# Part of the modulation's row sums of blocks 1 and 3: on GpSimd instead of TensorE

## The reference, cut to what matters

```
c_act = silu(c)                                   # 1024 values
mod = c_act @ w_ada + b_ada                       # w_ada: 1024 x 3072
shift, scale, gate = split(mod, 3)
u = layer_norm(x) * (1 + scale) + shift           # 512 x 1024
proj = u @ w_in + b_in                            # 1024 x 12288
```

## Time and profile before

| | us |
|---|---|
| median of 3 runs | 2165.53 (2165.42 to 2165.72) |
| profiled execution | 2165.25 |
| its span, first to last instruction | 2163.4 |
| PE busy in the span | 2140.2 (99%) |
| DVE busy | 1274.0 (59%) |
| POOL busy | 26.6 (1%), 41 instructions |

### The profile page before, as it was taken

How to read it: one execution, slowest core, us unless ns; L and a number is a source line. 1 busy time by engine, 2 the same in 40 slices (tenths; PEclk the granted TensorE clock), 3 DMA queues, 4 the chain that set the end, 5 groups by cost and what they waited for, 6 DMA issues and landing times.

```text
span 2163.4 us, 24967 instructions
## 1 busy us (share of the span) xinstructions
PE 2140.2 (99%) x10347; PEld 1765.4 (82%) x10347; DVE 1274.0 (59%) x1675; ACT 784.8 (36%) x1044; POOL 26.6 (1%) x41
## 2 busy tenths in 40 slices
PE   7999999999999999999999999999999999999998
PEld 4888888888888887888888888888788888888887
DVE  6899897944665848435665554234843576555423
ACT  3323232223343354344343333135534435333312
POOL 1000000000000100000000000000000000000000
PEclk9999999999999999999999999999999999999999
DMA  9432232332232222322223232222232222323322
GB/s 317 145 117 83 98 103 83 98 117 98 98 102 98 98 78 78 125 71 93 83 86 109 82 113 98 88 75 91 78 121 75 88 88 81 113 80 111 103 88 78
DMA packets 181588, 217.86 MB, mean 101 GB/s; under 512 B 3932, under 2 KB 153188, under 8 KB 181220
## 3 DMA queue, kind: packets, MB, share of 16 engines
q1 hardware_dynamic: 178080, 209.47, 29.0%
q10 hardware_dynamic: 2948, 4.65, 0.6%
q0 software_dynamic: 448, 2.15, 0.3%
HBM read 212.06 MB, written 4.19 MB: 100 GB/s over the span
## 4 chain that ended last, share of the span: by engine, by line
PE 94%; DVE 4%; issue 1%; ACT 1%; DMA 0%; POOL 0%; SPq 0%; POOLq 0%; ACTq 0%; DVEq 0%
PE psum L1821 30%; PE psum L1823 29%; PE psum L1822 29%; DVE whl L518 1%; PE psum L2236 1%; PE psum L2268 1%; PE psum L1964 1%; PE psum L2248 1%; PE psum L2202 1%; DMA ada<-in_w_ada 0%; PE psum L2189 0%; PE psum L2221 0%; PE psum L1845 0%; DVE mrow L1701 0%; POOL stat L682 0%
## 5 line engine op out<-in xcount | busy, mean ns | idle before, releaser
L1821 PE MATMUL psum<-hT,whl 128*128 128x512 f32 (+1 forms) x2064 | 789.2, 382 | 2.7 <-DVE whl L518 1.5
L1823 PE MATMUL psum<-hT,whl 128*128 128x512 f32 (+1 forms) x2064 | 783.2, 379 | 0.0
L1822 PE MATMUL psum<-hT,whl 128*128 128x512 f32 (+1 forms) x2064 | 783.0, 379 | 0.0
L518 DVE TENSOR_TENSOR whl<-raw,whl 128x1024 fp32r<-128x1024 f32 x361 | 438.4, 1217 | 428.3 <-ACT whl L511 428.1
L511 ACT ACTIVATE whl<-raw 128x1024 fp32r<-128x1024 f32 x361 | 376.6, 1047 | 421.8 <-PE psum L1823 387.0
L1821 PEld LDWEIGHTS psum<-hT,whl 128*128 128x128 f32 x2064 | 388.2, 188 | 84.5 <-issue 8.1
L1823 PEld LDWEIGHTS psum<-hT,whl 128*128 128x128 f32 x2064 | 388.2, 188 | 73.5
L1822 PEld LDWEIGHTS psum<-hT,whl 128*128 128x128 f32 x2064 | 388.3, 188 | 71.8 <-issue 0.2
L1821 PE MATMUL psum<-whl,ff 128*128 128x512 f32 x352 | 137.1, 389 | 0.0
L1823 PE MATMUL psum<-whl,ff 128*128 128x512 f32 x352 | 136.9, 389 | 0.0
L1822 PE MATMUL psum<-whl,ff 128*128 128x512 f32 x352 | 136.9, 389 | 0.0
(11 more groups left out here) (327 smaller groups left out, 2156.7 us busy)
## 6 DMA issues: line engine op xcount, KB each, us to landing
raw<-in_w_in SPq DMA_DIRECT2D x87, 1024.0 KB, 5.0
raw<-in_w_up SPq DMA_DIRECT2D x44, 1024.0 KB, 5.0
raw<-in_w_down SPq DMA_DIRECT2D x20, 1024.0 KB, 5.0
raw<-in_w_branch SPq DMA_DIRECT2D x12, 1024.0 KB, 5.1
raw<-in_w_out SPq DMA_DIRECT2D x12, 1024.0 KB, 5.0
ada<-in_w_ada SPq DMA_DIRECT2D x8, 1024.0 KB, 9.6
ada<-in_w_ada SPq DMA_DIRECT2D x8, 512.0 KB, 11.1
x<-in_x SPq DMA_DIRECT2D x4, 512.0 KB, 5.3
```

The lines of the kernel that those rows point to most:

```text
L518: nc.vector.tensor_tensor(whl_view(w, 1), raw_view(w), whl_view(w, 0).bitcast(F), ALU.subtract).then_inc(w_lo, 1)
L1821: M(out_, stat_hi, mov_hi, start=start, stop=False, **kw)
L1822: M(out_, stat_hi, mov_lo, start=False, stop=False, **kw)
L1823: return M(out_, stat_lo, mov_hi, start=False, stop=stop, **kw)
```

## The change

The two or three leading row blocks of blocks 1 and 3 are no longer multiplied on PE. POOL scales each by its column of `cact` and adds them up in a new tile, `pool_part` (128x512), at a place in the arena that nothing uses at this time. It does so right after L686. The first row block is scaled into `pool_part`, the others in place, and each is then added to it; POOL waits for each of its instructions before the next. DVE adds the whole tile to its own partial sums. POOL waits for DVE's addition of block 1 before it overwrites `pool_part` for block 3. Blocks 0 and 2 stay as they are.

```
-    PE_ROWS = {0: 3, 2: 4, 1: 2, 3: 3}
+    PE_ROWS = {0: 3, 2: 4}
+    POOL_ROWS = {1: 2, 3: 3}
+    LEAD_ROWS = {**PE_ROWS, **POOL_ROWS}
...
+    pool_part = over("pool_part", 80 * K, [P, SEQ])
...
+            def weighted_rows(i):
+
+                b = MOD_ORDER[i]
+                pool.wait_ge(s_ada[b][0], 16)
+                for k in range(POOL_ROWS[b]):
+                    if k == 0:
+                        pool.wait_ge(s_adsum, i)
+                        row = pool_part[:]
+                    else:
+                        row = ada_rows(b, k)
+                    nc.gpsimd.tensor_scalar(row, ada_rows(b, k), cact[:, k:k + 1], None, ALU.mult).then_inc(s_pool_row, 1)
+                    rows[0] += 1
+                    pool.wait_ge(s_pool_row, rows[0])
+                    if k:
+                        ins = nc.gpsimd.tensor_tensor(pool_part[:], pool_part[:], ada_rows(b, k), ALU.add)
+                        if k < POOL_ROWS[b] - 1:
+                            ins.then_inc(s_pool_row, 1)
+                            rows[0] += 1
+                            pool.wait_ge(s_pool_row, rows[0])
+                ins.then_inc(s_pool_part, 1)
...
                     nc.gpsimd.tensor_tensor(whl_view(0, 1)[:, 4:8, :], raw_view(0)[:, 4:8, :], whl_view(0, 0)[:, 4:8, :].bitcast(F),
                                             ALU.subtract).then_inc(w_lo, 1)
+                    weighted_rows(2)
+                    weighted_rows(3)
...
+                if b in POOL_ROWS:
+                    dve.wait_ge(s_pool_part, i - 1)
+                    V.tensor_tensor(part, part, pool_part[:], ALU.add).then_inc(s_adsum, 1)
+                    return
                 dve.wait_ge(arow_ps, i + 1)
...
-            ada_product(2)
             part_tile(2, range(4))
             part_tile(3, range(4))
-            ada_product(3)
             ada_columns(2)
```

More of the change, by code:

```diff
@@ L391, in build @@
         s_c, s_cT, u_act = sem("c_in"), sem("c_transposed"), sem("u_by_act")
+        s_pool_row, s_pool_part = sem("ada_pool_row"), sem("ada_pool_part")
         arow_ps, s_part, s_w0, s_fx, s_u0, s_nmr, s_xc = sem("ada_row_psum"), sem("ada_part"), sem("first_piece"), sem("first_columns"), sem("first_u"), sem("neg_mean_rstd"), sem("x_columns")
@@ L678, in _ @@
             pool.wait_ge(pool_chain, 1)
+            def weighted_rows(i):
[17 more added lines that the diff above has]
+                ins.then_inc(s_pool_part, 1)
+            rows = [0]
             for i_, (s, tb) in enumerate(ORDER):
@@ L1155, in ada_sum @@
                 part = adsum[:, 2 * b:2 * b + 2, :].rearrange("p a b -> p (a b)")
-                for k in range(PE_ROWS[b], KT):
-                    if k == PE_ROWS[b] and k < 4:
+                for k in range(LEAD_ROWS[b], KT):
+                    if k == LEAD_ROWS[b] and k < 4:
                         dve.wait_ge(s_ada[b][0], 16)
@@ L1160, in ada_sum @@
                         dve.wait_ge(s_ada[b][k // 2 - 1], 16)
-                    if k == PE_ROWS[b]:
+                    if k == LEAD_ROWS[b]:
                         ins = V.tensor_scalar(part, ada_rows(b, k), cact[:, k:k + 1], None, ALU.mult)
```

## The result

The changed kernel takes 2170.89 us (median of 11 runs, 2169.76 to 2172.55), the kernel before 2165.42 (11 runs, 2165.03 to 2165.72). The ratio is 1.0026, with a 95% interval from 1.0018 to 1.0034: slower by 5.5 us. The profiled execution took 2170.41 with a span of 2168.6, 5.2 more than before.

What follows compares the result with a forecast made beforehand. PE, busy 99%, was taken as the bound. Gate at 46.08 plus 6.78 of held DVE time is 52.86 against 49.05; 2165.25 plus 3.81, with 0.28 for the median, gives 2169.3 us, range 2166 to 2173.

Steps and rivals of the forecast that it cites:

- The removed work: PE's one-column products of blocks 1 and 3, at 34.43 and 41.94, no longer done: 4.48 us off PE.
- the baseline: Without POOL's interference, DVE's last addition ends at 46.03 and PE's second column multiplications start at 46.08: a gain of 2.97.
- one for one: Any shift of PE's second group of column multiplications (L1972) was taken to reach the kernel's end in full.
- the gate: Start of PE's second group of column multiplications (L1972), 49.05 before; forecast at 46.08 + 6.78 = 52.86, 3.81 us later.
- The price of a scale on POOL: A 128x512 scale on POOL, for which no row existed, taken as 0.9 us, between 0.55 and 1.28.
- What a POOL operation costs DVE: Each POOL operation within DVE's list holds DVE for its length less 0.15: addition 1.13, scale 0.75, sum 6.78 us.
- POOL itself isn't late: POOL's five block 3 operations alternate with DVE's and end while DVE has two multiply-adds left.
- the alternation read off 758.90: POOL's power at 758.90 waits for one DVE operation only, not the next, so the two engines were taken to alternate.
- Rival B, the clock: PE's clock falls in some 5.7 us of waiting at the gate, 2.4 us more after it: 2171.7; chance 0.42.
- Rival A: POOL and DVE barely slow each other; POOL's block 3 part ready about when DVE is; gain 2 to 3 us; chance 0.08.

Runs made afterwards that it cites:

- e2: Changed kernel with POOL's scales and additions left out, so nobody computes the leading row blocks of blocks 1 and 3; 2163.45 us.
- e9: Kernel before, plus POOL's five block 3 operations added behind its last power, where DVE is almost idle, to price each alone; span 2168.0 us.
- e1: Changed kernel, but DVE neither waits for POOL's partial sum nor adds it, while POOL still does all its work; 2167.73 us.
- e5: Changed kernel with 24 extra unused 128x512 matmuls on PE, filling its wait ahead of the second group of column multiplications; 2169.12 us.
- e3: Changed kernel, with PE also doing as many unused one-column products as were removed, at their old places; 2169.79 us.
- e4: Changed kernel, but POOL scales the first row block and sums in place, so block 3 doesn't wait for DVE's addition of block 1; 2169.25 us.
- e7: Changed kernel, but only block 3's leading row blocks go to POOL, as soon as their data are in; block 1's stay on PE; 2168.94 us.
- e10: Kernel before, without POOL, with all eight row blocks of block 1 summed by DVE and no PE product for that block; 2163.24 us.
- e8: Kernel before, without POOL, with one row block each of blocks 1 and 3 moved from PE to DVE; 2163.98 us.
- e6: Changed kernel, but only block 1's two leading row blocks go to POOL; block 3's three stay on PE; 2164.14 us.

## Why the prediction was right or wrong

**Direction and size.** A time slower by 3.8 us was forecast, 2169.3 in a range of 2166 to 2173; it was 2170.9, slower by 5.5. The chances put 0.51 on a time that can't be told from no change (up to 2169.9) and 0.47 on slower; it came out beyond 2169.9. The mechanism of the forecast was not the one that acted: the time is the sum of a miss and of a rival that came true.

**The removed work, the baseline, one for one.** Right. e2 has the gate at 46.16 where the text had 46.08, and the gate's shift reaches the end within 0.1 us in all ten kernels, once the low clock behind it is counted.

**The price of a scale on POOL.** Wrong: taken as 0.9, bounded by 0.55 and 1.28, measured 1.56 alone (e9). "It reads one tile where the other reads two" was the reason for the middle, and the upper bound rested on it as well. The scale is dearer than the two-input addition. The Trainium skill (GPSIMD Engine Reference, Engine selection) calls elementwise operations with two inputs about twice as slow on GpSimd as on VectorE and those with one input roughly line rate. For the addition the traces agree, 1.26 against DVE's 0.69; for this scale, with a factor per partition, they don't, 1.56 against DVE's 0.48.

**What a POOL operation costs DVE.** Wrong in size: its length less 0.15 was the rule, 6.78 us in all; DVE's list grew by 3.1. An addition does hold DVE to its end (DVE's scale at 34.83 took 1.54 instead of 0.48 and ended 0.29 after POOL's addition; the multiply-add at 46.80 took 1.63 instead of 0.75). A scale holds it only at its beginning: DVE's subtraction of 30.64 took 0.98 instead of 0.69 and ended at 31.62, while POOL's scale ran on to 31.96. e9 shows the same (1.18 instead of 0.75). So the first four scales cost DVE 0.3 to 0.4 each, not 0.75. The last scale of block 3 waited for DVE's last multiply-add and held nothing, and the last addition met no work of DVE. By instructions: 1.4 us for the scales (forecast 3.4) and 1.9 for the additions (forecast 3.4); 0.2 of that came back by an earlier start of the list and a closer gap in it. DVE's two scales, which read one SBUF tile each, were held too (1.54 and 0.83 instead of 0.48), so the prediction was right to spare them nothing. The Trainium skill's rule (SBUF — State Buffer, Who interferes with whom) that the later one is blocked for the whole of the earlier instruction holds here for the additions and not for the scales.

**"POOL itself isn't late."** Wrong, and this is the step that failed: the prediction itself names POOL's part coming after DVE's multiply-adds as the sign of its being wrong, and it came 2.8 us after them (51.21 against 48.43). The step rested on the two points above and on the alternation read off 758.90 in the earlier trace rows. At 41.20 POOL's first scale did not get in between DVE's two weight halves (40.95 and 42.09, no wait between them) but ended 1.34 behind the second, so it took 3.45. The alternation did hold elsewhere: in block 1 the scale of 32.05 got in between the two weight halves (it ended 1.35 behind the first, and the second took 1.63 instead of 1.22), and between the multiply-adds POOL got its turns too. Even with no wait for DVE at all POOL would have ended at 41.20 + 7.57 = 48.8, a little behind DVE's 48.43; at the 0.9 of the forecast for a scale it would have been 46.8. So the price of the scale and the lost turns are both in it.

**The gate.** 52.86 was forecast, 52.05 came: two errors, a DVE list too long by 3.7 us and a POOL chain too short, that met within 0.8 us. That is luck. e1 takes them apart: DVE's held time alone puts the gate at 49.55, POOL's chain adds 2.5.

**Rival B, the clock.** It had 0.42 and came true. I priced it at 2.4; it took 2.2 (e5 against the changed kernel: 4.29 and 6.52). The reason for holding it below the forecast was that no row showed a wait between 1 and 10 us; e1, e3, e4 and e7 now show the low level behind waits of 3.67, 2.35, 2.76 and 4.19. The Trainium skill's rule that an idle array falls back to the half clock (TensorE: Matmul & The Clock Gate, What's actually happening) agrees with the 0.50 from 52 to 56 us, and B should have been given the larger chance.

**Rival A** (no lock) falls in its form, but its second half, POOL's part ready no earlier than DVE's, was nearer to what happened than the forecast's.

## What to carry to other kernels

Before work is moved off the bound engine, read who is late next at the gate that follows, and price the mover by its own chain: a slow engine with five dependent operations is a latency, however idle it is. A wait that the move opens on PE can cost twice, by its length and by the low clock behind it; here 1.4 to 2.4 us more for standing still 2.4 to 6.1 us. And if two engines share a sum, look at what the sharing itself costs (here an addition of 0.7 us on DVE): giving one block to DVE whole (e10, 2163.24) was better than giving it a bit more of both (e8, 2163.98).

## What the runs showed of the hardware that I had not expected

- POOL's 128x512 float32 scale with a factor per partition: 1.56 us alone; its addition of two such tiles: 1.26 (e9).
- PE's clock is not settled by the program alone. Behind the same wait of about 1 us at 41 us the granted clock stayed at 1.00 in the changed kernel's profile and fell to 0.50 in that of e5. In e3, e4 and e5 the clock fell when PE was already at work again, in the changed kernel, e1 and e7 while it still waited at the gate. The changed kernel's runs spread over 2.8 us, and the two slowest (2172.35 and 2172.55) have the lowest mean granted clock, 0.996. Those of e6, e8 and e10, whose waits are 0.3 us or less there, spread over 0.4 to 0.5, those of the kernel before over 0.6 to 0.7 (1.2 in the series of e1 to e4, by one run of 31).
- Whether POOL gets a turn between two DVE instructions with no wait between them isn't settled by their kind. A scale that started 0.09 to 0.21 us before the first of two weight halves got in between them (32.05 in the changed kernel; 32.43 and 41.51 in e4). One that started 0.24 or 0.25 us after the beginning of the first had to let both pass, and took 3.45 to 3.47 (the changed kernel, e1, e3, e5, e7). Why is open: the one-element power of 758.90 started 0.17 us after DVE's instruction and got its turn behind it.
